# Eighty early expert blocks, POOL's products in two groups, and alternating expert blocks in a three-layer kernel

## The reference, cut to what matters

```python
w_log = -jax.nn.softplus(-(w0 + jnp.tanh(wd) @ w_up)) - 0.5
a = jax.nn.sigmoid(a0 + ad @ a_up)
```

```python
cand = sv[:, :, 0, :, None] + sv[:, :, 1, None, :]
top_s, pos = lax.top_k(cand, PEER_TOPK)
eidx = jnp.take_along_axis(cidx, pos, axis=-1)
gate = jax.nn.softmax(top_s, axis=-1)
act = gelu(einsum('thkd,td->thk', take(expert_u, eidx), xb))
out = einsum('thk,thkd->td', gate * act, take(expert_v, eidx))
```

## Time and profile before

| | us |
|---|---|
| median of 3 runs | 2878.73 |
| lowest and highest run | 2874.61, 2882.69 |
| profiled execution, its own time | 2882.82 |
| its span, first to last instruction | 2881.0 |
| PE busy in the span | 2710.3 |
| VectorE busy | 2243.1 |
| POOL busy | 1294.2 |
| ScalarE busy | 1208.4 |

### The profile page before, as it was taken

How to read it: one execution, slowest core, us unless ns; L and a number is a source line. 1 busy time by engine, 2 the same in 40 slices (tenths; PEclk the granted TensorE clock), 3 DMA queues, 4 the chain that set the end, 5 groups by cost and what they waited for, 6 DMA issues and landing times.

```text
span 2881.0 us, 36846 instructions
## 1 busy us (share of the span) xinstructions
PE 2710.3 (94%) x14355; PEld 2252.6 (78%) x14355; DVE 2243.1 (78%) x3556; ACT 1208.4 (42%) x1794; POOL 1294.2 (45%) x851
## 2 busy tenths in 40 slices
PE   8889999999999999999999889999999999999997
PEld 4567777767767788787788878998888888888875
DVE  3688888876878987657569999983777788889875
ACT  3234444433533466733333335664333333333344
POOL 2333333322234544204334664435766666667620
PEclk8999999999999999999999989999999999999998
DMA  7321111134422221023233445668999899999971
GB/s 270 110 70 52 52 52 52 52 114 135 142 93 73 81 66 45 30 88 110 88 103 103 130 131 171 210 222 323 365 366 369 306 335 333 328 332 335 325 248 37
DMA packets 161725, 492.94 MB, mean 171 GB/s; under 512 B 14992, under 2 KB 49808, under 8 KB 161424
## 3 DMA queue, kind: packets, MB, share of 16 engines
q1 hardware_dynamic: 124688, 356.36, 36.7%
q0 software_dynamic: 36864, 134.23, 12.5%
HBM read 442.30 MB, written 48.23 MB: 170 GB/s over the span
## 4 chain that ended last, share of the span: by engine, by line
PE 55%; DVE 24%; DMA 9%; ACT 5%; POOL 3%; issue 3%; SPq 0%; DVEq 0%; ACTq 0%; POOLq 0%
PE ps L799 15%; PE ps L801 14%; PE ps L800 14%; DMA ex<-in_ev,small 4%; DVE oh L2562 3%; DVE ex L1795 2%; DMA ex<-in_urow,small 2%; DVE ex L2596 2%; PE ps L976 1%; DVE oh L2559 1%; POOL ex L2850 1%; DVE oh L2557 1%; PE ps L996 1%; PE ps L950 1%; DVE wsp L1795 1%
## 5 line engine op out<-in xcount | busy, mean ns | idle before, releaser
L2683 POOL TENSOR_TENSOR wsp<-ring,wsp 128x1024 fp32r<-128x1024 f32 x211 | 530.1, 2518 | 850.6 <-ACT wsp L1305 816.3
L799 PE MATMUL ps<-hT,wsp 128*128 128x512 f32 (+1 forms) x2024 | 777.9, 384 | 62.9 <-POOL wsp L2683 47.1
L801 PE MATMUL ps<-hT,wsp 128*128 128x512 f32 (+1 forms) x2024 | 749.5, 370 | 0.0
L800 PE MATMUL ps<-hT,wsp 128*128 128x512 f32 (+1 forms) x2024 | 748.9, 370 | 0.0
L799 PEld LDWEIGHTS ps<-hT,wsp 128*128 128x128 f32 x2024 | 387.1, 191 | 132.2 <-issue 51.5
L801 PEld LDWEIGHTS ps<-hT,wsp 128*128 128x128 f32 x2024 | 386.6, 191 | 46.9
L800 PEld LDWEIGHTS ps<-hT,wsp 128*128 128x128 f32 x2024 | 387.7, 192 | 44.1 <-issue 5.0
L1305 ACT ACTIVATE wsp<-ring 128x1024 fp32r<-128x1024 f32 x312 | 326.9, 1056 | 165.6 <-PE ps L801 80.1
L799 PE MATMUL ps<-ex 128*128 128x512 f32 x606 | 239.8, 396 | 29.4 <-DVE ex L1795 26.8
L2850 POOL DMA_INDIRECT ex<-in_ev,small x128 | 192.2, 1501 | 109.9 <-DVE ex L2596 94.3
L2850 POOL DMA_INDIRECT ex<-in_urow,small x128 | 195.3, 1526 | 95.0 <-DVE small L2589 85.5
(11 more groups left out here) (430 smaller groups left out, 5000.1 us busy)
## 6 DMA issues: line engine op xcount, KB each, us to landing
ring<-in_eu SPq DMA_DIRECT2D x128, 512.0 KB, 4.3
ring<-in_ev SPq DMA_DIRECT2D x128, 512.0 KB, 6.8
ring<-in_ein SPq DMA_DIRECT2D x57, 512.0 KB, 3.5
gd<-oh SPq DMA_DIRECT2D x6, 4096.0 KB, 14.3
ex<-gd SPq DMA_DIRECT2D x32, 768.0 KB, 7.7
ring<-in_oin SPq DMA_DIRECT2D x39, 512.0 KB, 3.5
ring<-in_ada SPq DMA_DIRECT2D x30, 512.0 KB, 3.5
ex<-zd SPq DMA_DIRECT2D x18, 768.0 KB, 10.3
```

The source lines that it names most:

```text
L799: pe.matmul(out, W[0], R[0], start=first, stop=False)
L800: pe.matmul(out, W[0], R[1], start=False, stop=False)
L801: return pe.matmul(out, W[1], R[0], start=False, stop=last)
L2683: pool.tensor_tensor(s[:, 1, :], raw_of(i), s[:, 0, :].bitcast(F32), ALU.subtract).then_inc(pool_done, G.step("lo", i))
```

## The change

Six edits go together.

1. NPRE rises from 18 to 20: 80 early first products. The eight more lie in the product-key blocks: nine instead of seven in each (one ahead of `cand`, one after the fourth part of `best`). `SOFT` is the number of early blocks up to the end of those blocks.
2. POOL's eight products of half 1 are issued in two groups of four, at the pieces of half 1 and of half 0, with a `pre` between.
3. In the late rounds `z` and `v` alternate; in the early ones the gating pieces still come first. `gload` stands behind the first `v` of a round. The put-off gating is issued at the fourth `v`.
4. Slots: from the late rounds on, first products get slots 0 to 3 and second ones 4 to 7, and `slot_before` looks for the last unit in the same slot.
5. Row pieces: 1.2 instead of 1.1 per `v` in the early rounds, 1.8 instead of 1.75 in the late ones.
6. `lora` becomes two pieces, the first a little ahead of the second.

```diff
 TAPS = 31
-NPRE = 18
+NPRE = 20
 TURN = 4
...
 NG = 256
+SOFT = 4 + 4 * 9
 QT = 2
...
 PLACES = {
-    "first": (303, 346, 351, 359, 425, 425, 513, 523, 523, 523, 523, 523, 523, 810, 863, 872, 882),
-    "prep": (396, 432, 432, 461, 472, 569, 595, 656, 677, 742, 838, 840, 851, 926, 949, 979, 1005),
+    "first": (283, 303, 346, 351, 359, 425, 425, 513, 523, 523, 523, 523, 523, 523, 810, 863, 872, 882),
+    "prep": (372, 396, 432, 432, 461, 472, 569, 595, 656, 677, 742, 838, 840, 851, 926, 949, 979, 1005),
     "invert": (0, 24, 63, 101, 154, 218, 281, 305, 347, 385, 425, 459, 518, 521, 582, 630, 652, 702, 763, 817,
...
     def prep(c):
-        return [("lora", c), ("kn", c), *(("knr", c, i) for i in range(CH)), ("mix", c), ("decay", c),
+        return [("lora", c, 0), ("lora", c, 1), ("kn", c), *(("knr", c, i) for i in range(CH)), ("mix", c), ("decay", c),
                 *(("inv", c, i) for i in range(CH)), ("hats", c), ("bonus", c),
...
     for blk in range(4):
+        pre()
         order.append(("cand", blk))
...
             order.append(("best", blk, part))
-            if part < 3:
-                pre()
+            pre()
         order.append(("gates", blk))
...
     for c in range(NC - 1):
-        share = 1.1 if c < NPRE - 1 else 1.75
-        for z_ in zs(c + 1):
-            order.append(z_)
-            if z_[3] is not None:
+        share = 1.2 if c < NPRE - 1 else 1.8
+        if c < NPRE - 1:
+            order.extend(zs(c + 1))
+        for j in range(JC):
+            if c >= NPRE - 1:
+                order.append(("z", c + 1, j, unit("eu", (c + 1) * JC + j)))
                 feed(share)
-        if c + 2 < NC:
-            order.append(("gload", c + 2))
-        for j in range(JC):
             order.append(("v", c, j, unit("ev", c * JC + j)))
             feed(share)
+            if j == 0 and c + 2 < NC:
+                order.append(("gload", c + 2))
     while row[0] < NG:
...
                 return wsp[:, nth[n] % SLOTS, :, :]
-            j = (n - FIRST + TURN) % (SLOTS + MORE)
+            j = slot_of(n)
             return wsp[:, j, :, :] if j < SLOTS else more[:, j - SLOTS, :, :]
+
+        def slot_of(n):
+            at, j = divmod(n - FIRST + TURN, SLOTS + MORE)
+            return j if at < NPRE * JC // (SLOTS + MORE) else j // 2 + 4 * (j % 2)
 
...
             if n - FIRST >= SLOTS + MORE:
-                return n - SLOTS - MORE
-            j = (n - FIRST + TURN) % (SLOTS + MORE)
+                return next(k for k in range(n - 1, FIRST - 1, -1) if slot_of(k) == slot_of(n))
+            j = slot_of(n)
             return next((k for k in halved[-SLOTS:] if nth[k] % SLOTS == j), -1) if j < SLOTS else -1
...
         def pre_tile(j):
-            return (xz if j < 32 else xo if j < 62 else exg)[j % 2]
+            return (xz if j < SOFT else xo if j < SOFT + 30 else exg)[j % 2]
 
...
 
-            def lora(c):
+            def lora(c, i):
                 w.wait_ge(rw_in, 96)
                 w.wait_ge(scalar_done, A("wl"))
-                m = slice(c * 128, (c + 1) * 128)
-                out, free = prep_b.open(("wd", c), A, "wd", c)
+                m, p, nm = slice(c * 128, (c + 1) * 128), slice(64 * i, 64 * i + 64), ("wd", "aa")[i]
+                out, free = prep_b.open((nm, c), A, nm, c)
                 w.wait_ge(*free)
-                pe.matmul(out, lup[0:64, m], wl[0:64, :], start=True, stop=True).then_inc(tensor_done, T.step("wd", c))
-                out, free = prep_b.open(("aa", c), A, "aa", c)
-                w.wait_ge(*free)
-                pe.matmul(out, lup[64:128, m], wl[64:128, :], start=True, stop=True).then_inc(
-                    tensor_done, T.step("aa", c))
+                pe.matmul(out, lup[p, m], wl[p, :], start=True, stop=True).then_inc(tensor_done, T.step(nm, c))
 
...
 
-            def lora(c):
-                w.wait_ge(tensor_done, T("wd", c))
-                w.wait_ge(vector_done, V.was("pw", c - 1))
-                act.activation(wdT, prep_b.at["wd", c], ACT.Sigmoid, bias=col("w0", c)).then_inc(
-                    scalar_done, A.step("wd", c))
+            def lora(c, i):
+                if i == 0:
+                    w.wait_ge(tensor_done, T("wd", c))
+                    w.wait_ge(vector_done, V.was("pw", c - 1))
+                    act.activation(wdT, prep_b.at["wd", c], ACT.Sigmoid, bias=col("w0", c)).then_inc(
+                        scalar_done, A.step("wd", c))
+                    return
                 w.wait_ge(tensor_done, T("aa", c))
...
             def v(c, j, n):
-                if j == 0 and NPRE <= c + 1 < NC:
+                if j == 3 and NPRE <= c + 1 < NC:
                     gated(c + 1, JC - 1)
...
             def look(blk, half):
-                if half:
-                    oh4 = cand2.rearrange("p (h k a) -> p h k a", h=8, k=16)
-                    sx4 = sxf.rearrange("p (h two) k -> p h two k", two=2)
-                    w.wait_ge(vector_done, V("oh", blk, 1))
-                    for h in range(8):
-                        pool.tensor_tensor(oh4[:, h, :, :], oh4[:, h, :, :], sx4[:, h, 1:2, :].broadcast_to([128, 16, 16]),
-                                           ALU.mult).then_inc(pool_done, G.step("look", blk))
+                oh4 = cand2.rearrange("p (h k a) -> p h k a", h=8, k=16)
+                sx4 = sxf.rearrange("p (h two) k -> p h two k", two=2)
+                w.wait_ge(vector_done, V("oh", blk, 1))
+                for h in range(0, 4) if half else range(4, 8):
+                    pool.tensor_tensor(oh4[:, h, :, :], oh4[:, h, :, :], sx4[:, h, 1:2, :].broadcast_to([128, 16, 16]),
+                                       ALU.mult).then_inc(pool_done, G.step("look", blk))
 
...
             def v(c, j, n):
-                if j == 0 and NPRE <= c + 1 < NC:
+                if j == 3 and NPRE <= c + 1 < NC:
                     gated(c + 1, JC - 1)
...
                 for s in z_out:
-                    w.wait_ge(s, 16 * 16)
+                    w.wait_ge(s, 16 * (SOFT // 2))
                 sp.dma_start(iom, t["iom"].partition_broadcast(128)).then_inc(iom_in, 16)
```

## The result

The changed kernel takes 2887.22 us (median of 20 runs, 2878.24 to 2896.24) against 2877.78 us for the kernel before (20 runs, 2872.24 to 2884.10): a ratio of 1.0033, interval 1.0023 to 1.0042. It is slower by 0.3%, not faster by 0.7%. The profiled execution has a span of 2884.6 us, 3.6 us more than before.

A forecast was written before the change was run, and what follows sets the result against it. VectorE was taken to pace the product-key and late expert parts, PE the early experts. Experts -27, product-key stretch +10 and lora -4 summed to -21 us: 2858 us against the median, range 2830 to 2880.

The forecast's parts named there:

- the item on the slots: Expert rounds: slot change-over and later gate loads cost PE 0; any late load is covered by ScalarE's lead.
- the +6: Early experts: more bytes per round shrink ScalarE's lead over PE, +6 us, between 0 and +13.
- signs named for "wrong": Product-key blocks over 46 us; PE waits for low halves in the early part; late rounds under 35 or over 39 us.
- Late part: Late experts, 12 rounds for 14: -60 us, of which two rounds less at 37.2 us give -74.4.
- half a cheap round is lost: +2: End of the late experts: rows last for 11.5 of 12 rounds, before 13 of 14, costing +2 us.
- Alternation: Late experts: alternating first and second products changes nothing, 0 us, bounds -42 and +12.
- Rival 5: Late experts: alternation frees rounds to PE's 33 us, -42 us, 2816 us; chance 0.17 for this or a good part.
- Early part: Early experts: eight second products more at 4.15 us each, +33.2 us.
- Product-key stretch: Product-key blocks: VectorE meets POOL's low halves, while POOL's two groups remove PE's 7 us stop; +10 us, bounds 0 and +18.
- Rival 2: Product-key blocks: PE's 7 us stop on POOL's low half stays, blocks of 48 us, 2887 us; chance 0.11.
- Lora: Second small lora matmul: issuing the first earlier removes waits of 0.8 us, -4 us, between -6 and 0.
- Rivals 3 and 4: Rows pace the late part, 2875 us, chance 0.12; DMA bounds the early part, 2875 us, chance 0.1.

The follow-up runs named there:

- experiment 2: Changed kernel with the early rounds' gate loads issued ahead of the first second product: 2857.55 us, ratio 0.9918.
- experiment 5: Kernel before with only the early rounds' gate loads moved behind the first second product: 2891.62 us, ratio 1.0051.
- experiment 4: Changed kernel with the gate loads one product later still, behind a round's second second product: 2927.34 us, ratio 1.0171.
- experiment 1: Changed kernel with 1.1 instead of 1.2 row pieces per early second product: 2887.3 us, ratio 1.0029.
- experiment 3: Changed kernel with 1.1 row pieces per early product and the early gate loads ahead: 2858.4 us, ratio 0.9925.
- experiment 8: Changed kernel with the expert order, slots and gate loads of the kernel before, shares 1.1 and 1.8: 2872.07 us, ratio 0.9976.
- experiment 9: Kernel before with split lora, alternating blocks, matching slots and early gate loads ahead; 72 early blocks, one POOL group: 2860.86 us, ratio 0.9943.

## Why the prediction was wrong

**The step that failed** is the sentence on the gate load in the item on the slots: "If it comes late, VectorE's gating waits and the low halves behind it, which ScalarE's lead covers; counted in the +6." It treated the loads as late by some microseconds, once, with a lead to cover it. But the thing delayed decides when it is next issued. A lead is drawn on once, a loop takes its share in every round: with 18.56 us beside PE's 16.6 a round costs 2 us, so by this estimate the lead covered some five of 19 rounds and 14 paid (28 / 2). The time for the load was mis-sized too: not "three products (12 us)". The load can be issued only behind the low half that follows the gating, 7.6 us after the gating began (2186.06 to 2193.69), and of PE's 16.6 us that leaves 9.0 for a landing of 10.3. I had followed what waits for the load, down to VectorE's low halves, but not the next step,'s "SPq L2875 <- DVE ex L1795": what those low halves release is SP's queue, in which the load itself stands. The links of this leg were in rows that I had read, and its price was to be had as well: 10.3 us of landing and a gating section that the trace of before shows. The other leg I did not see at all: a gathered row issued at the same place holds the gating up in a round with five rows.

That the place of the gate loads turns the sign is shown by experiments 2 and 5, their loop by experiment 4, and that rows cost something only beside it by experiments 1 to 3. Why a row holds the gating up beside the late loads and not without them (the gather moves at the same time as the gate loads, or all of VectorE's work comes later) no run takes apart. One of the signs named for "wrong" is there, PE waits for low halves in the early part (L805 <- L1799 above).

**The other terms.** With the gate loads ahead the time is 2857.55 us, the 2858 of the forecast; that is chance, since the terms were off in both directions.

- **Late part**, forecast -60: -49.6 without alternation, but experiment 8 is not the forecast's case. At 1.1 rows per early product it has 7.6 rows more in the late part (76 x 0.1), and at 1.2 to 1.6 us a row (below) these are 9 to 12 us: with 1.2 rows it would be some -60 (an estimate; not run). By the traces two terms in it were off and nearly cancel: the +6 for the lead, which shows no cost (experiment 5), and "half a cheap round is lost: +2", which was too small. The last 60 us of the late part, before and in experiment 8:

```profile
2753.10:2813.10 60.00, 56.41 (x269) 47.89 (x267) 39.82 (x42) 28.58 (x41) 8.38 (x7) 0.97 0.62 207
```

```profile
2744.10:2804.10 60.00, 41.66 (x177) 31.19 (x175) 45.06 (x43) 21.01 (x30) 19.56 (x13) 0.91 0.67 237
```

  Before, the rows are used up with the last first product and PE runs its last round at pace. In experiment 8 they go on for 33 us behind it (2776.0, and 2743.4 for the last gelu), and PE makes 92 matmuls fewer in 60 us; at 0.22 us each (300 / 1352 of the late rounds before) that is some 20 us. Experiment 2, which alternates and has the rows of the forecast, makes 231, 38 fewer than before: some 8 us instead of the +2. This is read from traces; no run took it apart.
- **Alternation**, taken as 0 between -42 and +12: -9 to -14 us (experiments 8 and 9). Rival 5 was right in kind at a fifth to a third of its price. "The trace shows no such wait" was too strong: the earlier trace rows has waits of VectorE for gathers and of PE for low halves, though which of them alternation takes away is not shown.
- **Early part**, +33.2: +33.8 with the gate loads ahead.
- **Product-key stretch**, +10 with bounds 0 and +18: +13.4. The first block alone takes 6.6 us more. That the groups would take PE's stop away came true, but my reason for needing it did not: with one group the time is the same. Rival 2 falls for the same reason, as VectorE, not PE, sets the block.
- **Lora**, -4: -5 to -7.
- **Rivals 3 and 4.** A row more in the late part costs it 1.2 us (9.3 us for 7.6 rows, experiments 2 and 3) or 1.6 us (11.8, the changed kernel and experiment 1), nearer the 1.30 of the earlier trace rows than 2.66: rows do not pace the late part. DMA does not bound the early part. The Trainium skill (SBUF — State Buffer, section "A bandwidth-pool intuition that's wrong (but worth ruling out)") gives HBM about 358 GB/s per core; the trace of experiment 2 shows 368 GB/s over 160 us with PE at full pace, so by measurement that figure is no ceiling here.

Moved blocks and groups together were to bring -27 + 10 = -17 us, and brought 0 to -7 (experiments 8 and 9); the range had no case in which a load that is moved closes a loop.

## What to carry to other kernels

When a piece that issues a DMA is moved in an in-order queue, look at the instruction just ahead of it: if that waits for a buffer, follow who frees it, and if the freeing work stands behind the use of the moved load, there is a loop, whose round (landing plus all work between) has to be set against the stage's round, not against a lead. An even fall of every engine's busy share was its mark here, and putting one more step into it tested it. Read the chain of waits over all rounds, not over one: here two legs of nearly the same length closed the loop, and the one that was first looked at was the rarer.

## What the runs showed of the hardware

**VectorE is held up in single-input instructions too.** In the fourth block of the changed kernel, VectorE and then POOL in order of time:

```profile
1709.82 1.49 DVE L2470 TENSOR_SCALAR pk<-pk 128x128 uint32<-128x128 uint32 x1
1711.34 0.23 DVE L2472 CAST pk<-pk 128x128 f32<-128x128 uint32 x1
...
1712.52 6.71 DVE L2484 TENSOR_TENSOR pk<-pk 128x2048 f32<-128x2048 f32 x2
```

```profile
1708.83 2.39 POOL L2687 TENSOR_TENSOR wsp<-ring,wsp 128x1024 fp32r<-128x1024 f32 x1 [1.76 <-ACT wsp L1307]
1712.99 8.49 POOL L2687 TENSOR_TENSOR wsp<-ring,wsp 128x1024 fp32r<-128x1024 f32 x2 [1.77 <-ACT wsp L1307]
```

The 0.23 us instruction ends at 1711.31, just after POOL's low half (1708.83 + 2.39 = 1711.22); another of that kind took 2.40 us. The two one-hot compares take 6.71 us beside a low half and 4.62 us without, and the two low halves 8.49 us, where the median of one is 2.40. I had counted only the products, the candidate sums and the gate product as exposed; these others may be what made +13.4 of the +10, which no run took apart. The Trainium skill (SBUF — State Buffer, section "SBUF: two separate sides") has VectorE and GpSimd share one port pair under a lock held for a whole instruction, which VectorE's two-input operations and its two-port modes take; the end of the held instruction at the end of the low half agrees. Whether that instruction runs in such a mode no run shows.

**DMA** moved 368 GB/s at a share of 0.98 for 160 us beside a PE that never waited; the best 40 us of the kernel before had 371.
